# Queries and gates of a recurrence as seven half-size products, and state-space tiles activated as they are projected

## The chip, the cores and the metric

One NeuronCore of a Trainium2 chip runs the whole program. The metric is the device time of one execution in microseconds. Five engines work side by side: TensorE (PE, with its weight loads PEld), VectorE (DVE), ScalarE (ACT), GpSimd (POOL) and SyncE (SP), which here only issues transfers.

## The reference, cut to what matters

The program is three transformer-like blocks over 512 tokens of width 1024. The change lies in the third, all in fp32:

```
h = rmsnorm(x) * (1 + scale1) + shift1
z, xbc, dt, q, f_fwd, f_bwd, i, g = split(h @ w_in)
# state-space half
xbc = silu(conv5(xbc) + conv_b)                 # 1536 columns: 1024 x, 256 b, 256 c
y = x * d_skip + scan(x, b, c, dt) + reversed scan
y_ssd = rmsnorm(y * silu(z))
# gated linear recurrence half, for each direction d with f = f_fwd, f_bwd
log_f = logaddexp(log(lb), log1p(-lb) + log_sigmoid(f));  k = (1 - lb) * sigmoid(-f)
S_t = diag(f_t) S_{t-1} + k_t v_t^T;  o_t = S_t^T q_t           # v = i
y_hg = rmsnorm(o_fwd + o_bwd) * silu(g)
x = x + gate1 * (concat(y_ssd, y_hg) @ w_out)
```

`h @ w_in` for q and for g are two products of 1024 x 1024 by 1024 x 512 (features by tokens).

## The kernel before, in words

Activations lie in SBUF as tiles of 128 features by 512 tokens: `hT` is the normed input in eight such tiles, `xT` the residual stream. A `Stream` brings weights in pieces of 2 MB into two places; a piece is loaded into a place when the products that read the piece before it there are done (`products_to`). Each stage is a block: every engine has its own instruction list, the engines meet by semaphores, and a barrier stands at a block's end. Semaphores of closed blocks are cleared in bulk, with a barrier, when over 80 are used up (L126 to L136).

**State-space inputs** (`ssd_inputs`, L3196). TensorE makes twelve products (L3237) in eight PSUM banks; ScalarE copies each into a padded tile `raw` (L3252); VectorE does the convolution, one multiply and four multiply-adds a tile (L3269, L3272). When all twelve copies are issued, ScalarE applies Silu to the twelve tiles (L3257). Then a block of its own, `ssd_prepare` (L3287), turns the eight x tiles and two b tiles by transposes (L3308, L3311), makes the scores b'c (L3314), has ScalarE copy the twelve results out (L3321), and VectorE write `y = x * skip` (L3326). Two `ssd_direction` blocks follow.

**Inputs of the recurrence** (`hgrn_inputs`, L3517). TensorE makes five products of 8 banks each, in the order forget, back-forget, value, query, gate: a bank is 8 tiles of contraction (16 matmul records of 512 columns, L3578). ScalarE takes each bank to SBUF by `take` (L3587). Between the takes stand the steps of a chain that makes log f and k, first for one direction and then for the other: Abs, Exp, Ln, Abs, Exp, Exp of the kept part, Ln (L3594 to L3626), with VectorE's steps between (L3678 to L3703). The chain's scratch tiles `a` and `b` are the tiles of the gates and of the queries. So a query bank is taken only when VectorE has counted `done` for its tile (L3701), the last but one step of the second direction's chain, which goes tile by tile. The kept parts go to DRAM through a ring of two tiles by transfers that GpSimd issues (L3554); ScalarE waits for the ring.

**After it**: `hgrn_recurrence` (L3706), sixteen passes, during which SyncE loads a 256 KB row block `kept` for each pass two passes ahead; then `mixed_out` (L4006).

**`SevenProducts`** (L225) is used in `mixed_out` and elsewhere. A pair of output tiles (256 features by 512 tokens, contraction 1024) is split in halves each way and made by seven products of half size instead of eight: each is 4 tiles of contraction by 256 columns. Products 5, 6 and 7 need sums of weight quarters s1 to s4 (`weigh`, four VectorE operations of 128 x 512) and sums of input quarters t1 to t4 (`add_values`, one operation of 128 x 1024 each); product 4 needs t4, product 3 needs s4. ScalarE takes product 1 (`first_out`) and products 1+2 (`corner_out`); VectorE adds the rest (`join_first`, three operations, and `join_last`, two). Pairs listed in `whole` are made plainly; a pair in `eager` runs its products in the order 1, 2, 6, 7, 5, 4, 3, others 1, 6, 7, 5, 2, 4, 3. Pair n uses banks 4(n mod 2) to 4(n mod 2) + 3.

Of the kernel before, what the change touches and what calls it, by code (L numbers as in the profile page):

```python
# [22 lines left out]
P = 128  # L23
# [3172 lines left out]
def ssd_inputs(core, stream, hT, conv_w, conv_b, xbc, normed, steps, z_load):  # L3196
# [6 lines left out]
    PIECES = TILES // 4  # L3203
    with ExitStack() as ctx:
        (raw,) = bufs(nc, ctx, "si", raw=[P, XT, T + 2 * PAD])
        product = stream.product
        copied, padded, tap, convolved, activated = sems(
            nc, ctx, *(f"si_{s}" for s in ("copied", "padded", "tap", "convolved", "activated")))
# [15 lines left out]
        @block.tensor  # L3224
        def _(pe):
            for n in normed:
                n.sums(pe)
            steps.multiply(pe, hT, B[7], normed[-1])
            for n in range(TILES):
                if n % 4 == 0:  # L3230
                    w = stream.take(pe)
                if n == 7:
                    pe.wait_ge(steps.copied, 1)
                if n >= 8:
                    pe.wait_ge(copied, n - 7)
                for k in range(KT):
                    mm = nc.tensor.matmul(B[n % 8][:], w[:, k, (n % 4) * P:(n % 4 + 1) * P], hT[:, k, :],  # L3237
                                          start=(k == 0), stop=(k == KT - 1))
                mm.then_inc(product, 1)
                if n == 10:  # L3240
                    pe.wait_ge(copied, 10)
                    steps.turn(pe, B[0], B[1])

        @block.scalar
        def _(act):
            for n in normed:
                n.scalar(act)
            steps.take(act, B[7])
            steps.logs(act)
            for n in range(TILES):  # L3250
                act.wait_ge(product, n + 1)
                nc.scalar.copy(raw[:, n, PAD:PAD + T], B[n % 8][:]).then_inc(copied, 1)  # L3252
                if n == 3:
                    steps.decays(act)
            for n in range(XT):
                act.wait_ge(convolved, n + 1)
                nc.scalar.activation(xbc[:, n, :], xbc[:, n, :], ACT.Silu, bias=conv_b[:, n:n + 1]).then_inc(activated, 1)  # L3257

        @block.vector
        def _(dve):  # L3260
# [6 lines left out]
            for n in range(XT):  # L3267
                dve.wait_ge(copied, n + 1)
                nc.vector.tensor_scalar(xbc[:, n, :], raw[:, n, 0:T], conv_w[:, n, 0:1], None, ALU.mult).then_inc(tap, 1)  # L3269
                for j in range(1, SSD_CONV):  # L3270
                    dve.wait_ge(tap, (SSD_CONV - 1) * n + j)
                    nc.vector.scalar_tensor_tensor(  # L3272
                        out=xbc[:, n, :], in0=raw[:, n, j:j + T], scalar=conv_w[:, n, j:j + 1], in1=xbc[:, n, :],
                        op0=ALU.mult, op1=ALU.add).then_inc(convolved if j == SSD_CONV - 1 else tap, 1)
                if n == 3:
                    steps.weigh(dve)
            steps.place(dve, B[0], B[1])

# [6 lines left out]


def ssd_prepare(core, xbc, x_tm, b_tm, scores, y, skip, ident):  # L3287

    nc = core.nc
    B = core.bank  # L3290
    with ExitStack() as ctx:
        turned, copied, skipped = sems(nc, ctx, "sp_turned", "sp_copied", "sp_skipped")
        block = ctx.enter_context(nc.Block())

        outs = [(x_tm[:, n // 2, (n % 2) * 512:(n % 2 + 1) * 512]) for n in range(8)]
        outs += [b_tm[:, 2 * n:2 * n + 2, :].rearrange("p t c -> p (t c)") for n in range(2)]
        outs += [scores[:, g, :] for g in range(SSD_G)]

        @block.tensor
        def _(pe):  # L3300
            for n in range(12):
                if n >= 8:
                    pe.wait_ge(copied, n - 7)
                for j in range(4):
                    out = B[n % 8][:, j * P:(j + 1) * P]
                    if n < 8:
                        t, k = n // 2, 4 * (n % 2) + j
                        mm = nc.tensor.transpose(out, xbc[:, k, t * P:(t + 1) * P], ident[:])  # L3308
                    elif n < 10:
                        t, g = 2 * (n - 8) + j // 2, j % 2  # L3310
                        mm = nc.tensor.transpose(out, xbc[:, 8 + g, t * P:(t + 1) * P], ident[:])  # L3311
                    else:
                        g, cols = n - 10, slice(j * P, (j + 1) * P)
                        mm = nc.tensor.matmul(out, xbc[:, 8 + g, cols], xbc[:, 10 + g, cols], start=True, stop=True)  # L3314
                mm.then_inc(turned, 1)

        @block.scalar
        def _(act):
            for n in range(12):
                act.wait_ge(turned, n + 1)  # L3320
                nc.scalar.copy(outs[n], B[n % 8][:]).then_inc(copied, 1)  # L3321

        @block.vector
        def _(dve):
            for k in range(KT):
                nc.vector.tensor_scalar(y[:, k, :], xbc[:, k, :], skip[:, k:k + 1], None, ALU.mult).then_inc(skipped, 1)  # L3326
# [190 lines left out]
def hgrn_inputs(core, stream, hT, f, q, gate, v_tm, K, total, lower, y_ssd, zs, ssd_gain, ones, kept_dram):  # L3517
# [9 lines left out]
    with ExitStack() as ctx:  # L3527
# [6 lines left out]
         kept_log, apart, joined, logged, summed, totalled, shifted, done) = sems(  # L3534
# [3 lines left out]
                "shifted", "done")))  # L3538
        block = ctx.enter_context(nc.Block())
        base = stream.base()  # L3540
        FORGET, BACK, VALUE, QUERY, GATE = range(5)

        @block.sync
# [15 lines left out]
        def _(pe):  # L3559
            for i in range(5):  # L3560
                for s in range(2):
                    w = stream.take(pe)
                    for m in range(4):
# [15 lines left out]
                        mm.then_inc(stream.product, 1)  # L3579

        @block.scalar
        def _(act):
# [66 lines left out]
            for n in range(8):  # L3649
                act.wait_ge(done, n + 1)  # L3650
                take(QUERY, n, q[:, n, :], ACT.Identity)
            for n in range(8):
                act.wait_ge(joined, KT + n + 1)
                take(GATE, n, gate[:, n, :], ACT.Silu)

        @block.vector
        def _(dve):
# [14 lines left out]
            for d in range(2):  # L3672
# [12 lines left out]
                for k in range(KT):  # L3685
# [20 lines left out]
def hgrn_recurrence(core, q, sums, keys, totals, v_tm, y, ident, kept_dram, ahead):  # L3706
# [14 lines left out]
    with ExitStack() as ctx:  # L3721
# [5 lines left out]
         turned_copied, u_made, state, out_made, added, cleared, *kept_loaded) = sems(  # L3727
            nc, ctx, *(f"{name}_{s}" for s in (
                "loaded", "negated", "diffed", "q_exped", "k_exped", "scaled", "product", "picked", "zeroed", "started", "decayed", "end_diffed",
                "end_exped", "end_scaled", "turned", "turned_copied", "u_made", "state", "out_made", "added", "cleared",  # L3730
# [16 lines left out]
        def _(sp):  # L3747
            for d, levels in enumerate(("levels", "levels_back")):
                sp.dma_start(mask[:, d], core.const(levels)).then_inc(loaded, 16)
            for h in range(PASSES):  # L3750
                if h >= 2:
                    sp.wait_ge(product, NM * (h - 1))
                if h == HG_H + 2:
                    ahead(sp)
                sp.dma_start(kept[:, h % 2, :], kept_rows(kept_dram, h // HG_H, h % HG_H)).then_inc(kept_loaded[h % 2], 16)

# [438 lines left out]
def third_block(core, a, xT, hT, ident, ones, out):  # L4195
    nc = core.nc
    w_in = a["w_in_3"][0]
    with ExitStack() as ctx:
# [5 lines left out]
        hin = Stream(core, hin_ctx, "hin", 2, halves(w_in[:, 1024 + XBC + SSD_H:], (1, 2, 3, 0, 4)), first=zw[:])  # L4204
# [16 lines left out]
        with ExitStack() as s:  # L4221
            (ycat,) = bufs(nc, s, "b3", ycat=[P, 2 * KT, T])
            y_ssd, y_hg = ycat[:, 0:KT, :], ycat[:, KT:2 * KT, :]
            with ExitStack() as r:
                (zs,) = bufs(nc, r, "b3", zs=[P, KT, T])
                with ExitStack() as q:
                    xbc, *by_token = bufs(nc, q, "b3", xbc=[P, XT, T], dT=[P, TT, SSD_ROWS], shift=[P, TT, SSD_ROWS],
                                          WT=[P, TT, SSD_ROWS], CD=[P, TT, SSD_ROWS])
                    with ExitStack() as n:
# [5 lines left out]
                        ssd_inputs(core, si, hT, c["conv_w"], c["conv_b"], xbc, (n8, n9), steps, z_load)  # L4235
                    si_ctx.close()
                    b_tm, scores = bufs(nc, q, "b3", b_tm=[P, TT, SSD_G * P], scores=[P, SSD_G, T])
                    x_tm = y_hg.rearrange("p (t a) c -> p t (a c)", a=2)
                    ssd_prepare(core, xbc, x_tm, b_tm, scores, y_ssd, c["skip"], ident)
# [4 lines left out]
                with ExitStack() as q:  # L4244
                    ff, fb, kf = bufs(nc, q, "b3", ff=[P, KT, T], fb=[P, KT, T], kf=[P, KT, T])
                    v_tm = y_hg.rearrange("p (t a) c -> p t (a c)", a=2)
                    f, K, total = (ff, fb), (kf, zs), (c["total"], c["back_total"])
                    hgrn_inputs(core, hin, hT, f, hq, gs, v_tm, K, total, lower, y_ssd, zs, c["ssd_norm_w"], ones,
                                a["y_dram"])
# [7 lines left out]
                    hgrn_recurrence(core, hq, f, K, total, v_tm, hT, ident, a["y_dram"], first_out)  # L4257
# [34 lines left out]
def build(nc, a, out):  # L4292
    USED.clear()
    with ExitStack() as ctx:
# [13 lines left out]
        core.bias_stored, core.small_loaded, core.rest_loaded = (  # L4308
            ctx.enter_context(nc.semaphore(n)) for n in ("bias_stored", "small_loaded", "rest_loaded"))
# [35 lines left out]
```

## Time and profile before

| | us |
|---|---|
| median of 3 runs (lowest, highest) | 3619.79 (3616.84, 3621.1) |
| the profiled execution | 3621.61 |
| its span | 3619.4 |
| PE busy in the span | 3346.4 (92%) |
| DVE busy | 1600.5 (44%) |
| ACT busy | 765.7 (21%) |
| POOL busy | 266.4 (7%) |

The mean granted clock of TensorE was 0.95 of full speed. The span is the time from the first to the last instruction of the profiled execution; the rest lies around it. Times in the rows below count from the span's start.

### The profile page before, as it was taken

The page shows a single profiled execution, that of the slowest core. Times are in us where ns is not written, and L with a number is a line of the kernel's source. Part 1 is how long each engine was busy: PE and PEld are TensorE (multiplying, and loading weights), DVE is VectorE, ACT ScalarE, POOL GpSimd, SP SyncE. Part 2 cuts the span into 40 slices and gives each one's busy share as a digit, 9 for nine tenths or more (in the row PEclk, how much of TensorE's full clock was granted, in tenths as well). Part 3 has the DMA queues.
Part 4 walks back from the last instruction along what each step waited for, and adds up shares of the span by engine and source line. Part 5 has one row for each costly group of instructions (what it writes and reads, how often), then busy time and mean ns, then how long its engine had stood idle before and what let it go on. Part 6 is the DMA issues. An engine that isn't in the chain of part 4 may idle for free. (4 is left out here: it accounts for less than half of the span.)

```text
span 3619.4 us, 35011 instructions
## 1 busy us (share of the span) xinstructions
PE 3346.4 (92%) x12642; PEld 1891.8 (52%) x12642; DVE 1600.5 (44%) x2838; ACT 765.7 (21%) x1556; POOL 266.4 (7%) x372
## 2 busy tenths in 40 slices
PE   8995599999997899999999999698999998989998
PEld 3443247544474344444444444335544498868886
DVE  6882715893355111111111110556526288644553
ACT  1102312112113011010010010225544266120001
POOL 1000021000001000000000000100000187000000
PEclk9995699999998999999999999799999999999998
DMA  8860028212115999999999995413323101312220
GB/s 264 300 211 25 14 108 317 80 70 70 47 53 210 399 401 400 397 393 398 396 394 401 394 393 220 146 48 94 120 95 115 34 25 39 131 69 71 93 94 24
DMA packets 204253, 683.62 MB, mean 189 GB/s; under 512 B 15974, under 2 KB 27832, under 8 KB 171356
## 3 DMA queue, kind: packets, MB, share of 16 engines
q1 hardware_dynamic: 179340, 607.83, 44.7%
q0 software_dynamic: 14576, 48.71, 3.8%
q10 hardware_dynamic: 10208, 25.37, 1.9%
q8 instruction: 80, 1.31, 0.2%
q14 instruction: 49, 0.40, 0.0%
HBM read 628.63 MB, written 53.23 MB: 188 GB/s over the span
## 5 line engine op out<-in xcount | busy, mean ns | idle before, releaser
L2604 PE MATMUL bank<-moe_gu,all_hT 128*128 128x512 f32 x1024 | 445.2, 595 | 10.6 <-PEq L136 9.4
L2886 DVE TENSOR_SCALAR all_hT<-bank 128x512 f32<-128x512 f32 x48 | 33.2, 692 | 798.9 <-PE bank L2610 637.4
L2604 PEld LDWEIGHTS bank<-moe_gu,all_hT 128*128 128x128 f32 x1024 | 195.3, 191 | 256.2 <-issue 254.8
L2626 PE MATMUL bank<-moe_gu,all_hT 128*64 128x512 f32 x1024 | 222.6, 592 | 1.5 <-issue 1.5
L1922 PE MATMUL bank<-all_hT,early_w 128*128 128x512 f32 x512 | 220.2, 592 | 0.0
L2646 PE MATMUL bank<-moe_dn,moe_rows 128*128 128x512 f32 x480 | 210.0, 595 | 4.2 <-ACT moe_rows L2781 4.2
L1922 PEld LDWEIGHTS bank<-all_hT,early_w 128*128 128x128 f32 x512 | 97.3, 190 | 122.0 <-issue 122.0
L1984 DVE SCALAR_TENSOR_TENSOR b_conv<-conv_ya,all_table,b_conv 128x512 f32<-128x512 f32 x240 | 159.4, 748 | 0.0
L2626 PEld LDWEIGHTS bank<-moe_gu,all_hT 128*64 128x64 f32 x1024 | 76.4, 137 | 144.8 <-issue 144.8
L2646 PEld LDWEIGHTS bank<-moe_dn,moe_rows 128*128 128x128 f32 x480 | 90.0, 190 | 115.3 <-issue 107.6
L3956 PE MATMUL bank<-hg_qs,hg_ks 128*128 128x64 f32 x896 | 114.3, 279 | 19.7 <-ACT hg_ks L3845 13.8
L3956 PEld LDWEIGHTS bank<-hg_qs,hg_ks 128*128 128x128 f32 x896 | 110.9, 199 | 22.2 <-ACT hg_ks L3845 15.3
L3578 PE MATMUL bank<-all_hT,z_w 128*128 128x512 f32 x256 | 112.9, 602 | 4.8 <-PEq L3339 4.8
L397 PE MATMUL bank<-b_v,ff_S 128*128 128x256 f32 x496 | 117.2, 379 | 0.0
L3578 PE MATMUL bank<-all_hT,hin_w 128*128 128x512 f32 x256 | 110.5, 592 | 0.0
L2664 PE MATMUL bank<-moe_dn,all_hT 128*64 128x512 f32 x480 | 106.3, 595 | 0.8 <-ACT all_hT L2785 0.8
L1191 PE MATMUL bank<-all_hT,early_w 128*128 128x512 f32 x224 | 104.3, 624 | 0.8 <-DVE all_hT L800 0.8
L397 PEld LDWEIGHTS bank<-b_v,ff_S 128*128 128x128 f32 x496 | 94.2, 190 | 12.8
L2963 POOL DMA_INDIRECT combine_rows<-expert_rows,ex_row x16 | 17.6, 1102 | 1115.0 <-SPq L2948 1110.5
L2785 ACT COPY all_hT<-bank 128x512 f32<-128x512 f32 x16 | 9.4, 587 | 424.0 <-PE bank L2556 424.0
L3578 PEld LDWEIGHTS bank<-all_hT,z_w 128*128 128x128 f32 x256 | 49.5, 194 | 67.1 <-issue 67.1
L3237 PE MATMUL bank<-all_hT,si_w 128*128 128x512 f32 x192 | 82.9, 593 | 0.0
(837 smaller groups left out, 5389.2 us busy)
## 6 DMA issues: line engine op xcount, KB each, us to landing
moe_gu<-in_w_gu_dram SPq DMA_DIRECT2D x128, 2048.0 KB, 14.6
moe_dn<-in_w_dn_dram SPq DMA_DIRECT2D x62, 2048.0 KB, 14.2
early_w<-in_w_in_dram SPq DMA_DIRECT2D x13, 2048.0 KB, 9.0
expert_rows<-b_z POOLq DMA_DIRECT2D x49, 512.0 KB, 20.5
mods_w<-in_w_mod_dram SPq DMA_DIRECT2D x48, 512.0 KB, 5.3
mods_w<-in_ada_w_dram SPq DMA_DIRECT2D x48, 512.0 KB, 5.1
late_w<-in_w_up_dram SPq DMA_DIRECT2D x8, 2048.0 KB, 9.0
late_w<-in_w_down_dram SPq DMA_DIRECT2D x8, 2048.0 KB, 7.8
```

The lines of the kernel that those rows point to most:

```text
L397: mm = self.nc.tensor.matmul(self.bank(n, into), left[:, k, :], right[:, k, :], start=start and k == 0, stop=not start and k == 3, skip_gr ...
L1191: mm = nc.tensor.matmul(bank[:], w[:, k, at:at + P], hT[:, k, :], **flags)
L1922: mm = nc.tensor.matmul(bank(n)[:], w[:, k, (n % 4) * P:(n % 4 + 1) * P], hT[:, k, :], start=(k == 0), stop=(k == KT - 1))
L1984: nc.vector.scalar_tensor_tensor(out=conv[:, k, :], in0=ya[:, k, bass.ds(j, T)], scalar=conv_w[:, k, bass.ds(j, 1)], in1=conv[:, k, :], op ...
L2604: mm = nc.tensor.matmul(B[bank][:], xb2[:, k, :], gu[:, q, kk, col:col + HALF], start=(k == 0), stop=False)
L2626: mm = nc.tensor.matmul(B[bank][part, :], xb1[:, k % 4, k // 4, :], gu[:, 4 + q, kk, col + h * HALF:col + (h + 1) * HALF], start=(k == 0), ...
L2646: mm = nc.tensor.matmul(B[2 + n][:], left[:, k * P:(k + 1) * P], dn[:, c, j * D + n * HALF:j * D + (n + 1) * HALF], start=(k == 0), stop=( ...
L2664: mm = nc.tensor.matmul(B[4][part, :], hidT1[:, j, c, :], w[:, c, j * D + h * HALF:j * D + (h + 1) * HALF], start=(c == 0 and j == 0), sto ...
L2886: vec.tensor_scalar(g, gate[:], SWIGLU_LIMIT, None, ALU.min).then_inc(clipped, 1)
L3237: mm = nc.tensor.matmul(B[n % 8][:], w[:, k, (n % 4) * P:(n % 4 + 1) * P], hT[:, k, :], start=(k == 0), stop=(k == KT - 1))
L3578: mm = nc.tensor.matmul(B[n][:], left, right, start=(k == 0), stop=(k == KT - 1))
L3956: mm = nc.tensor.matmul(B[n % 4][:, c * w:(c + 1) * w], left[:, c * P:(c + 1) * P], right[:, c * w:(c + 1) * w], start=True, stop=True)
```

## The change

1. **Queries and gates.** In `hgrn_inputs` TensorE's plain loop stops after three products (forget, back-forget, value). Query and gate become eight pairs of a `SevenProducts`: pairs 0 and 1 (query tiles 0 to 3) plain, pairs 2 to 7 by seven products, pair 2 in the eager order. Pair 0 waits for 20 and pair 1 for all 24 of the banks taken before. The input sums are written over `y_ssd`'s first six tiles, the half sums over its last two, and the weight sums over `xT`. Both are stored to DRAM first: `xT` (2 MB) by SyncE at the block's start, ahead of the weight pieces; `y_ssd` (2 MB) by GpSimd when it is normed, ahead of the kept parts on GpSimd's queue. SyncE brings them back in the recurrence when its second and its third pass are done, each ahead of a `kept` row block. VectorE's sums stand in its list behind the whole chain of the second direction. The gate's Silu becomes an operation on the joined tile.
2. **State-space tiles.** Silu moves between the copies: tiles 0 to 3 after copy 4, tile n - 1 after copy n. `raw` has 8 tiles in place of 12. The block `ssd_prepare` is gone; its transposes, scores and copies run at the end of `ssd_inputs`, on six banks, one x tile after the other (the copy writes four pieces of 128 columns), and its `y = x * skip` behind VectorE's convolution. The last tile's Silu stands behind four of the copies.

```diff
 # ssd_inputs, TensorE, after the twelve products
+            for i in range(len(outs)):
+                if i < len(TURN_BANKS):
+                    pe.wait_ge(copied, max(n for n in range(TILES) if n % 8 == TURN_BANKS[i]) + 1)
+                else:
+                    pe.wait_ge(turned_copied, i - len(TURN_BANKS) + 1)
+                pe.wait_ge(activated, i + 1)
...
 # ssd_inputs, ScalarE
             for n in range(TILES):
                 act.wait_ge(product, n + 1)
-                nc.scalar.copy(raw[:, n, PAD:PAD + T], B[n % 8][:]).then_inc(copied, 1)
+                if n >= RAW:
+                    act.wait_ge(convolved, n - RAW + 1)
+                nc.scalar.copy(raw[:, n % RAW, PAD:PAD + T], B[n % 8][:]).then_inc(copied, 1)
                 if n == 3:
                     steps.decays(act)
-            for n in range(XT):
-                act.wait_ge(convolved, n + 1)
-                nc.scalar.activation(xbc[:, n, :], xbc[:, n, :], ACT.Silu, bias=conv_b[:, n:n + 1]).then_inc(activated, 1)
+                if n >= 4:
+                    for m in range(4) if n == 4 else [n - 1]:
+                        activate(m)
+            for i in range(len(outs)):
+                if i == LAST_AFTER:
+                    activate(TILES - 1)
+                act.wait_ge(turned, i + 1)
+                nc.scalar.copy(outs[i], turn_bank(i)[:].rearrange("p (t c) -> p t c", c=P)).then_inc(turned_copied, 1)
 # hgrn_inputs, SyncE and GpSimd
+            sp.dma_start(x_away, xT.rearrange("p k t -> p (k t)")).then_inc(x_stored, 16)
             stream.load(sp, 10)
+            pool.wait_ge(ssd_normed, KT)
+            pool.dma_start(y_away, y_ssd.rearrange("p k t -> p (k t)")).then_inc(core.y_ssd_stored, 16)
 # hgrn_inputs, TensorE
-            for i in range(5):
+            for i in range(3):
...
+            for n in range(own.count):
+                if n < 2:
+                    pe.wait_ge(copied, 2 * KT + 4 * (n + 1))
+                if n in own.whole:
+                    own.multiply_whole(pe, n)
+                else:
+                    own.multiply(pe, n, own.order(n))
 # hgrn_inputs, ScalarE, after the values
-            for n in range(8):
-                act.wait_ge(done, n + 1)
-                take(QUERY, n, q[:, n, :], ACT.Identity)
-            for n in range(8):
-                act.wait_ge(joined, KT + n + 1)
-                take(GATE, n, gate[:, n, :], ACT.Silu)
+            for n in own.whole:
+                act.wait_ge(done, 2 * n + 2)
+                own.whole_out(act, n)
+            for n in range(2, own.count):
+                own.first_out(act, n)
+                act.wait_ge(done, min(2 * n + 2, KT))
+                own.corner_out(act, n)
+                if n > 4:
+                    open_gate(n - 1)
+            open_gate(own.count - 1)
 # hgrn_inputs, VectorE, after the loop over both directions
+            dve.wait_ge(x_stored, 16)
+            dve.wait_ge(core.y_ssd_stored, 16)
+            for i in (0, 1, 3):
+                own.add_values(dve, 0, i)
+            own.weigh(dve, 2)
+            own.weigh(dve, 3)
+            dve.wait_ge(stream.product, own.base + 2)
+            own.add_values(dve, 0, 2)
+            for n in range(2, own.count):
+                own.join_first(dve, n)
+                own.join_last(dve, n)
+                if n + 2 < own.count:
+                    own.weigh(dve, n + 2)
 # hgrn_recurrence, SyncE, in the loop over passes
+                if h in (3, 4):
+                    to, away = back[h - 3]
+                    sp.dma_start(to.rearrange("p k t -> p (k t)"), away).then_inc(brought_back, 16)
```

`open_gate(n)` waits for the joined tiles of pair n and applies Silu to both.

## Rows read from the trace of the kernel before

**Rows 1.** windows: busy us of PE, PEld, DVE, ACT, POOL by stage, then clock
```profile
2452.10:2472.60 20.50, 8.86 (x57) 8.66 (x56) 7.81 (x17) 15.97 (x26) 0.00 (x0) 0.67 0.00 0
...
2590.50:2877.50 287.00, 284.07 (x656) 125.47 (x656) 101.08 (x157) 107.40 (x180) 8.79 (x17) 0.99 0.24 82
```

**Rows 2.** timeline, TensorE, inputs of the recurrence: start, duration, instruction, idle before
```profile
2593.11 30.00 PE L3578 MATMUL bank<-all_hT,z_w 128*128 128x512 f32 x64 [4.78 <-PEq L3339]
...
2739.68 27.63 PE L3578 MATMUL bank<-hin_w,all_hT 128*128 128x512 f32 x64
...
2767.15 27.63 PE L3578 MATMUL bank<-all_hT,z_w 128*128 128x512 f32 x64
...
2849.55 27.63 PE L3578 MATMUL bank<-all_hT,hin_w 128*128 128x512 f32 x64
```

**Rows 3.** timeline, VectorE, second direction's chain
```profile
2785.91 0.69 DVE L3688 SCALAR_TENSOR_TENSOR b_hq<-b_hq,b_gs 128x512 f32<-128x512 f32 x1 [26.35 <-ACT b_gs L3626]
...
2818.20 0.69 DVE L3703 TENSOR_TENSOR b_zs<-b_fb,b_zs 128x512 f32<-128x512 f32 x1
```

**Rows 4.** timeline, ScalarE, same stage: ring wait, last values, end
```profile
2775.05 0.63 ACT L3621 ACTIVATE hgate_kept<-b_zs 128x512 f32<-128x512 f32 x1 [7.24 <-DMA expert_rows<-hgate_kept]
...
2789.42 1.06 ACT L3587 ACTIVATE b_ycat<-bank 128x512 f32<-128x512 f32 x2
...
2877.28 0.60 ACT L3587 ACTIVATE b_gs<-bank 128x512 f32<-128x512 f32 x1 [6.27 <-PE bank L3578]
```

**Rows 5.** windows, TensorE after an idle stretch: busy us, granted clock, DMA
```profile
2593.00:2595.00 2.00, 1.89 (x3) 0.50 0.43 96
```

**Rows 6.** timeline, VectorE, sums of a seven-product stage after the recurrence
```profile
3072.60 0.69 DVE L431 TENSOR_TENSOR mx_S<-first_out_w 128x512 f32<-128x512 f32 x1 [1.54 <-PEq L136]
...
3074.53 0.69 DVE L436 TENSOR_TENSOR mx_S<-first_out_w,mx_S 128x512 f32<-128x512 f32 x1
...
3075.14 1.22 DVE L450 TENSOR_TENSOR b_zs<-b_ycat 128x1024 f32<-128x1024 f32 x1
...
3078.67 1.22 DVE L461 TENSOR_TENSOR b_zs<-b_ycat,b_zs 128x1024 f32<-128x1024 f32 x1
```

**Rows 7.** timeline, TensorE, first products of two consecutive pairs there
```profile
3143.66 1.89 PE L397 MATMUL bank<-b_ycat,late_w 128*128 128x256 f32 x8
...
3155.75 1.89 PE L397 MATMUL bank<-b_ycat,late_w 128*128 128x256 f32 x8
```

**Rows 8.** DMA issues of the page and of the inputs stage: KB each, us to landing
```profile
expert_rows<-b_z POOLq DMA_DIRECT2D x49, 512.0 KB, 20.5
...
expert_rows<-hgate_kept POOLq DMA_DIRECT2D x16, 256.0 KB, 2.3
```

**Rows 9.** timelines, VectorE and GpSimd: state-space result normed, first kept part stored
```profile
2635.47 5.39 DVE L3667 SCALAR_TENSOR_TENSOR b_ycat<-b_ycat,all_table,hgate_rstd 128x512 f32<-128x512 f32 x8
...
2697.28 1.15 POOL L3554 DMA_DIRECT2D expert_rows<-hgate_kept  x2 [104.11 <-ACT hgate_kept L3621]
```

**Rows 10.** timeline, all engines, end of the state-space inputs and the turning block
```profile
2452.18 0.59 ACT L3252 COPY si_raw<-bank 128x512 f32<-128x512 f32 x1 [8.24 <-PE bank L3237]
...
2453.32 3.11 DVE L3272 SCALAR_TENSOR_TENSOR b_xbc<-si_raw,all_table,b_xbc 128x512 f32<-128x512 f32 x4
...
2454.07 7.45 ACT L3257 ACTIVATE b_xbc<-b_xbc,all_table 128x512 f32<-128x512 f32 x12
...
2457.14 0.35 DVE L3193 COPY b_CD<-bank 128x192 f32<-128x192 f32 x1
...
2462.93 6.17 PE L3308 MATMUL bank<-all_ident,b_xbc 128*128 128x128 f32 x32 [10.80 <-PEq L136]
...
2462.94 3.26 DVE L3326 TENSOR_SCALAR b_ycat<-b_xbc,all_skip 128x512 f32<-128x512 f32 x8 [5.45 <-PEq L136]
...
2472.69 3.67 PE L3475 MATMUL bank<-all_hT,z_w 128*128 128x512 f32 x8 [0.93 <-PEq L3291]
```

**Rows 11.** timeline, SyncE's queue, same stage
```profile
2767.34 0.37 SPq L193 DMA_DIRECT2D hin_w<-in_w_in_dram  x1
```

More of the change, by code:

```diff
@@ L3242, in _ @@
                     steps.turn(pe, B[0], B[1])
+            for i in range(len(outs)):
[4 more added lines that the diff above has]
+                pe.wait_ge(activated, i + 1)
+                for t in range(TT):
+                    out, cols = turn_bank(i)[:, t * P:(t + 1) * P], slice(t * P, (t + 1) * P)
+                    if i < KT + SSD_G:
+                        mm = nc.tensor.transpose(out, xbc[:, i, cols], ident[:])
+                    else:
+                        mm = nc.tensor.matmul(out, xbc[:, i - SSD_G, cols], xbc[:, i, cols], start=True, stop=True)
+                mm.then_inc(turned, 1)
         @block.scalar
@@ L3277, in _ @@
             steps.place(dve, B[0], B[1])
+            for k in range(KT):
+                dve.wait_ge(activated, k + 1)
+                nc.vector.tensor_scalar(y[:, k, :], xbc[:, k, :], skip[:, k:k + 1], None, ALU.mult).then_inc(skipped, 1)
 def ssd_pieces(w_in):
@@ L3284, in ssd_pieces @@
     return [(v[:, :, col:col + HALF], 4) for col in cols]
[L3287 to L3326, printed above, removed]
 def ssd_direction(core, d, xbc, x_tm, b_tm, scores, columns, y, rows_dram, hT, zw, z_loaded, z_load, zs):
@@ L3537, in hgrn_inputs @@
                 "outer_term", "log_sig", "kept_log", "apart", "joined", "logged", "summed", "totalled",
-                "shifted", "done")))
-        block = ctx.enter_context(nc.Block())
+                "shifted", "done", "opened")))
+        (x_stored,) = sems(nc, ctx, "hgate_x_stored")
         base = stream.base()
         FORGET, BACK, VALUE, QUERY, GATE = range(5)
+        units = [dict(src=hT, into=lambda n: q[:, n % KT, :]), dict(src=hT, into=lambda n: gate[:, n % KT, :])]
+        own = SevenProducts(core, ctx, stream, "hgate", units, (SevenProducts.weights_within(xT),
+                                                                *SevenProducts.parts_within(y_ssd[:, 6:8, :])),
+                            (SevenProducts.values_within(y_ssd[:, 0:6, :]),), eager=[2], whole=[0, 1])
+        own.base, own.pieces = base + 3 * KT, stream.taken + 6
+        block = ctx.enter_context(nc.Block())
         @block.sync
@@ L3648, in _, with open_gate @@
                 take(VALUE, n, v_tm[:, n % 4, n // 4 * HALF:(n // 4 + 1) * HALF], ACT.Identity)
-            for n in range(8):
-                act.wait_ge(done, n + 1)
-                take(QUERY, n, q[:, n, :], ACT.Identity)
-            for n in range(8):
-                act.wait_ge(joined, KT + n + 1)
-                take(GATE, n, gate[:, n, :], ACT.Silu)
+            def open_gate(n):
+                own.joined(act, n)
+                for i in range(2):
+                    tile = own.units[n // 4]["into"](2 * n + i)
+                    func(tile, tile, ACT.Silu).then_inc(opened, 1)
+            for n in own.whole:
[8 more added lines that the diff above has]
+            open_gate(own.count - 1)
         @block.vector
```

57 lines of the change are left out of this document (37 added, 20 removed).

## The prediction

> **What bounds the kernel now.** I read the table of windows by stage first. TensorE sets the time almost everywhere, and the two stages that the change touches are opposites. In the turning block between the state-space inputs and the two directions TensorE is busy for 8.86 of 20.5 us; in the inputs of the recurrence it is busy for 284 of 287 us [rows 1]. So the first has time to give back by being laid beside other work, and the second by less TensorE work, as long as nothing else becomes late there.
>
> The engines' timelines of the second stage come next. TensorE runs its five products without a gap, four banks in 27.47 us (2767.15 - 2739.68), so a pair of banks takes 13.73 us; the last product starts its second half at 2849.55 and ends 27.47 us later, at 2877.02 [rows 2]. Beside it runs the chain for the forget gates, which is not bound by TensorE: VectorE starts its last part, eight tiles one after the other, at 2785.91 when ScalarE's last logarithm arrives, and ends at 2818.89 [rows 3]. The chain thus ends 58 us before TensorE does, and all of the query and gate work after 2767.15 is what hides it. ScalarE takes the queries as the chain frees their tiles, behind the last values at 2789.42 [rows 4]; that banks come round only every eighth product keeps this from TensorE.
>
> **Queries and gates, step by step**, in the clock of the trace before.
>
> - *Pair 0* runs plainly from 2767.15 to 2780.9.
> - *Pair 1* waits until all 24 banks are taken. The last two values are taken at 2789.42 to 2790.48, because the ring of kept parts and the last logarithms stand before them in ScalarE's list [rows 4]. TensorE idles 9.6 us, then works to 2804.2. After 4.78 us of idling its half clock (0.50) made four banks take 30.00 instead of 27.6 us [rows 2, 5]; with 2.4 us for that, pair 1 ends at 2806.6, and products 1 and 2 of pair 2, with ScalarE's copy between, at about 2810.5.
> - *Product 6 of pair 2* needs t2 and s2, which VectorE makes only behind the chain. It is busy to 2818.89. Three input sums, at the pace of the same sums in the later stage, take 3.53 us (3075.14 to 3078.67), to 2822.4; s1, s3 and s2 take 1.93 us (3072.60 to 3074.53), to 2824.3 [rows 3, 6]. So TensorE idles a second time, for 13.8 us. This wait swallows the one before pair 1 and its slow restart whole: neither is counted.
> - *Product 7* needs t3, which stands behind both sets of weight sums: 2 x 2.54 us from 2822.4, then 1.22, gives 2828.7 [rows 6]. Products 7, 5, 4 and 3 then take 4 x 1.73 us, since a pair's seven take 12.09 us (3155.75 - 3143.66) [rows 7]. That is 2835.7. The restart at half clock covers product 6, which has 4.4 us of room, and may reach into product 7: between 0 and 2.4 us by [rows 2, 5], of which I take 1.0, as much of it lies in the room. Pair 2 ends at 2836.7.
> - *Pairs 3 to 7*: 5 x 12.09 = 60.45 us, to 2897.1. VectorE needs about 5 us of each 12 for the joins (five additions of 0.4) and the next weight sums (2.54), and ScalarE under 3, so I add no wait; the weight pieces have some 24 us each.
> - *Tail*: before, one Silu of 0.60 us follows the last bank [rows 4]; now one VectorE addition (I take 0.4, half of the columns of a 0.69 operation [rows 6]) and two Silus follow: 1.0 us more.
>
> TensorE ends at 2897.1 instead of 2877.0, so the stage is longer by 20.1 + 1.0 = **21.1 us**. Seen as a balance: six pairs save 6 x (13.73 - 12.09) = 9.8 us of work; two idle stretches, the wait for t3 and restarts cost about 30.
>
> A rule of the Trainium skill speaks against the change here too: TensorE: Matmul & The Clock Gate, section HAM oscillation, says that idle gaps between bursts of matmuls put the engine back to half rate, so that a restart is paid after each. By it both gaps would cost a restart; the trace agrees for one gap (0.50 after 4.78 us). With the second restart at its full 2.4 us the sum would be 1.4 us higher, without any it would be 1.0 lower.
>
> *Transfers.* The store of `xT` stands ahead of the weight piece at 2593, which is not needed before TensorE has made four banks, 30 us later [rows 2]. The store of `y_ssd` stands on GpSimd's queue ahead of the kept parts. Its 2 MB bound from below by eight times the 256 KB that land in 2.3 us, 18 us, and from above by four times the 512 KB that took 20.5 us in the busiest stage, 82 us [rows 8]. The room is 56 us, from the last normed tile at 2635.47 + 5.39 = 2640.9 to the first kept part at 2697.3 [rows 9], so I take the near row, from this stage, and count nothing. The Trainium skill, DMA: Bandwidth & Descriptors, section on the anatomy of a DMA, gives a fit for GpSimd-issued copies, 2.0 us plus bytes over 436 000; that is an estimate of 6.8 us, and no delay either. In the recurrence the two loads of 2 MB precede row blocks that are needed a whole pass after the next; nothing counted, at most some us if they were late.
>
> **State-space tiles.** Before, the last Silu ends at 2454.07 + 7.45 = 2461.52, the barrier of the clearing costs 1.4 us, the turning block runs from 2462.93, and the first direction starts TensorE at 2472.69 [rows 10]. After, TensorE can turn tiles from 2452.2 on. ScalarE takes the last product to 2452.77, one Silu (0.62 at the row's pace) to 2453.4, four copies of 0.55 to 2455.6, waits for the last convolution, which ends at 2453.32 + 3.11 = 2456.43, makes its Silu to 2457.1 and eight copies of 0.55, to 2461.5 [rows 10]. VectorE places its four small copies (the last ends by 2457.5) and then needs 3.26 us for the skip, to 2460.8 [rows 10]. So the block ends when it ended before, and the turning block from 2462.93 to 2472.69 falls away: **-9.8 us**. The earlier Silus and their table load lie in ScalarE's idle time between the copies (8.24 us before the last [rows 10]). The barrier of the clearing moves on to the first direction; a second such barrier moves from the entry of `mixed_out` to that of the recurrence, for nothing. If the four-piece copies were slower, or TensorE restarted at half clock after its 3 us without work, up to 2.4 us of the gain are lost.
>
> **Sum.** 3621.6 + 21.1 - 9.8 = 3632.9 us against the profiled execution. The median of the runs is 1.8 us lower, so I forecast 3631 us, 11 us slower.
>
> **Rivals.**
>
> - *The sums come in time and TensorE stays the bound* (faster). Then the six pairs give back 9.8 us, the turning block 9.8, the tail costs 1.0: 3619.8 - 18.6 = 3601. It decides at about 2810: VectorE's sums would have to be made 14 us earlier. For it speaks that VectorE stands idle for 26.35 us before 2785.91; against it, that its list is in order and the sums stand behind the chain [rows 3]. Chance 0.09, with what I may have overlooked in that direction.
> - *The chain ends earlier.* ScalarE waits 7.24 us for the ring at 2775.05, because a weight piece was issued at 2767.34, just before the kept part [rows 4, 11]. With other transfers around it that wait may shrink, at most to nothing: the whole stage follows the chain now, so up to 7.2 us come off, 3624 to 3627, within 0.2% of before. The piece is still released by the end of the values, so little speaks for it. Chance 0.10.
> - *The store of `y_ssd` is late.* At 82 us it ends at about 2723, 26 us after the first kept part, which waits behind it, and the chain with it: 3657. Against it the row of this stage [rows 8]. Chance 0.03.
> - *The turning block's work does not fit* and its time is paid in the longer block: 3641. Chance 0.04.
>
> **How the numbers follow.** The forecast has 0.74, with a range of its own from 3627 to 3635: 1.0 less and 1.4 more for the restart, 2.4 for the turning block, about 2 for the runs' own spread. A measurement of this kernel can tell about 0.2%, 7.2 us, from no change. Faster: 0.09. Same: the shorter chain, 0.10, and the forecast's low edge, 0.05. Slower: the rest, 0.76. The range goes from 3622, through the shorter chain, to 3638, through half of the turning block's rival.
>
> **What would show it.** Right: in TensorE's timeline two gaps in the query stage, the longer one ended by VectorE's weight sums; the chain's last operation as late after the stage's start as before (226 us); six pairs of 12.1 us; the stage some 21 us longer; the first direction 9.8 us earlier after the last state-space product. Wrong: no second gap, or the sums ahead of the chain's end; a transfer as the releaser of a kept part beyond 7 us; the recurrence longer by more than 2 us; or copies of the turned tiles well over 0.6 us.

## The result, and the profile after

The changed kernel's median is 3627.9 us (14 runs, 3619.2 to 3631.8) against 3616.8 us of the kernel before on the same chip (14 runs): a ratio of 1.0027, 95% interval 1.0020 to 1.0035. That is 11.1 us slower, where 3631 us and 11.3 us slower had been forecast. Of the 3.1 us between 3631 and 3627.9, 3.0 come from the base: the kernel before has a median of 3616.8 us here and had 3619.8 in the three runs from which the forecast went out. The profiled execution took 3628.9 us, with a span of 3627.1.

First the windows of the two stages that the change touches, as in [rows 1], and TensorE's window behind the second gap, to set beside [rows 5] (stretch, its length, busy us of PE, PEld, DVE, ACT and POOL with their counts, granted clock, DMA share, GB/s).

```profile
2449.40:2459.90 10.50, 6.53 (x57) 6.11 (x56) 7.72 (x17) 7.75 (x15) 0.00 (x0) 1.00 0.00 0
...
2579.60:2885.60 306.00, 280.05 (x800) 154.72 (x800) 131.27 (x212) 109.51 (x188) 9.32 (x18) 0.96 0.26 90
...
2810.50:2812.50 2.00, 1.96 (x5) 1.60 (x6) 1.98 (x4) 0.00 (x0) 0.00 (x0) 0.50 0.00 0
```

The state-space stage's end has shrunk from 20.5 to 10.5 us. The inputs of the recurrence have grown from 287 to 306 us although TensorE is busy for 4 us less in them: what the longer stage holds is idle time.

TensorE's timeline of the query and gate products shows it (start, duration, instruction, and in brackets the idle time before and what ended it). [Rows 2] had no idle time here.

```profile
2753.99 13.90 PE L352 MATMUL bank<-all_hT,z_w 128*128 128x512 f32 x32
2776.69 17.05 PE L352 MATMUL bank<-all_hT,z_w 128*128 128x512 f32 x32 [8.80 <-ACT b_ycat L3597]
2793.57 1.89 PE L397 MATMUL bank<-all_hT,hin_w 128*128 128x256 f32 x8
2795.93 1.99 PE L397 MATMUL bank<-all_hT,hin_w 128*128 128x256 f32 x8 [0.46 <-ACT b_ycat L405]
2810.54 3.47 PE L397 MATMUL bank<-b_ycat,all_xT 128*128 128x256 f32 x8 [12.62 <-DVE all_xT L434]
2815.03 1.97 PE L397 MATMUL bank<-all_hT,all_xT 128*128 128x256 f32 x8 [1.01 <-DVE all_hT L458]
...
2822.01 1.89 PE L397 MATMUL bank<-all_hT,hin_w 128*128 128x256 f32 x8
...
2880.71 1.89 PE L397 MATMUL bank<-all_hT,all_xT 128*128 128x256 f32 x8
```

The values end at 2753.99, pair 0 runs, and TensorE waits 8.80 us for ScalarE's last value copy. It then does pair 1 and two products of pair 2, and waits 12.62 us for the weight sum s2 on VectorE and 1.01 us more for t3. From 2822.01 on there is no idle time: the five pairs 3 to 7 take 60.4 us, to 2882.44. Read as a balance, the eight pairs took 109.9 us before (2877.02 - 2767.15) and take 128.45 now. Six pairs save 9.8; the four idle stretches add 22.9; half clock after them adds 3.15 to pair 1 and 1.6 to product 6; 0.8 is left for modelled ends and slightly longer first products.

VectorE's timeline names the cause of the long gap; compare [rows 3, 6].

```profile
2772.07 0.69 DVE L3708 SCALAR_TENSOR_TENSOR b_hq<-b_hq,b_gs 128x512 f32<-128x512 f32 x1 [25.98 <-ACT b_gs L3636]
...
2804.34 0.69 DVE L3723 TENSOR_TENSOR b_zs<-b_fb,b_zs 128x512 f32<-128x512 f32 x1
2804.95 1.22 DVE L450 TENSOR_TENSOR b_ycat<-all_hT 128x1024 f32<-128x1024 f32 x1
...
2807.46 1.22 DVE L461 TENSOR_TENSOR b_ycat<-all_hT,b_ycat 128x1024 f32<-128x1024 f32 x1
2808.60 0.68 DVE L431 TENSOR_TENSOR all_xT<-hin_w 128x512 f32<-128x512 f32 x1
...
2809.81 0.68 DVE L434 TENSOR_TENSOR all_xT<-all_xT,hin_w 128x512 f32<-128x512 f32 x1
...
2813.66 1.22 DVE L458 TENSOR_TENSOR all_hT<-all_hT 128x1024 f32<-128x1024 f32 x1
...
2882.64 0.42 DVE L485 TENSOR_TENSOR b_gs<-b_ycat,bank 128x256 f32<-128x256 f32 x1 [1.30 <-PE bank L397]
```

VectorE idles 25.98 us before the chain's last part, makes the chain without a break to 2805.03, and only then the input sums (L450 to L461) and the weight sums (L431 to L436). TensorE's product 6 starts 0.05 us after the sum of L434 is made. The chain ends 225.4 us after the stage's first product, where it ended 225.8 after it before.

ScalarE in the same stage, beside [rows 4]: the wait for the ring of kept parts, the last two values, and the end.

```profile
2759.36 0.63 ACT L3631 ACTIVATE hgate_kept<-b_zs 128x512 f32<-128x512 f32 x1 [5.02 <-DMA expert_rows<-hgate_kept]
...
2775.58 1.05 ACT L3597 ACTIVATE b_ycat<-bank 128x512 f32<-128x512 f32 x2
...
2883.18 1.15 ACT L3663 ACTIVATE b_gs<-b_gs 128x512 f32<-128x512 f32 x2 [2.52 <-DVE b_gs L485]
2885.63 1.28 ACT L3832 ACT_TABLE_LOAD   x1 [1.31 <-PEq L136]
```

The ring's wait is 5.02 us instead of 7.24. At the end two Silus follow the last join, and then 1.31 us of the semaphore-clearing barrier; the recurrence's first instruction comes 3.2 us behind TensorE's end, where it came 1.1 us behind it.

The moved transfers, from the DMA issues of the stretch from 2570 to 3080 (KB each, us to landing).

```profile
expert_rows<-all_xT SPq DMA_DIRECT2D x1, 2048.0 KB, 8.8
h_rows<-b_ycat POOLq DMA_DIRECT2D x1, 2048.0 KB, 6.6
all_xT<-expert_rows SPq DMA_DIRECT2D x1, 2048.0 KB, 8.0
b_ycat<-h_rows SPq DMA_DIRECT2D x1, 2048.0 KB, 7.6
```

All four land in under 9 us; none of them ends a wait in the timelines above.

The turning block, all engines, beside [rows 10].

```profile
2449.35 4.53 PE L3259 MATMUL bank<-all_ident,b_xbc 128*128 128x128 f32 x40
2449.55 0.59 ACT L3280 COPY si_raw<-bank 128x512 f32<-128x512 f32 x1 [7.63 <-PE bank L3244]
...
2450.66 2.04 ACT L3290 COPY b_ycat<-bank 128x512 f32<-128x512 f32 x4
...
2453.84 0.72 ACT L3272 ACTIVATE b_xbc<-b_xbc,all_table 128x512 f32<-128x512 f32 x1 [1.15 <-DVE b_xbc L3305]
...
2457.32 1.12 ACT L3290 COPY b_scores<-bank 128x512 f32<-128x512 f32 x2
...
2459.93 3.67 PE L3469 MATMUL bank<-all_hT,z_w 128*128 128x512 f32 x8 [2.79 <-PEq L136]
```

TensorE turns tiles directly behind the last product, ScalarE's copies of the turned tiles take 0.51 us each (2.04 / 4), and the first direction starts 10.38 us after the start of the last product's copy (2459.93 - 2449.55), where it was 20.51 (2472.69 - 2452.18).

Put together, stage by stage, from the two profiled executions:

| stretch | before | after | difference | forecast |
|---|---|---|---|---|
| up to the first state-space product (not touched) | 2367.5 | 2364.9 | -2.6 | 0 |
| from there to the last state-space copy | 84.7 | 84.7 | 0.0 | 0 |
| last state-space copy to first direction | 20.51 | 10.38 | -10.1 | -9.8 |
| the two directions | 120.4 | 119.7 | -0.7 | 0 |
| inputs of the recurrence, TensorE's start to end | 283.9 | 302.8 | +18.9 | +20.1 |
| from there to the recurrence's first instruction | 1.1 | 3.2 | +2.1 | +1.0 |
| rest of the span | 741.3 | 741.5 | +0.2 | 0 |

Without the first line, which lies ahead of the change and is between 2359 and 2368 us in all the profiled executions of this study, the sum is +10.4 us; the medians differ by 11.1, the forecast was +11.3.

### The profile page after: what moved, and what is told of

The parts are those of the page before. It is cut to its first block and busy times, and to the rows that moved or that the text cites. A ratio compares the mean times of both kernels' runs of the same rounds, so it can differ in the third digit from the quotient of the medians.

```text
span 3627.1 us, 35437 instructions
## 1 busy us (share of the span) xinstructions
PE 3338.8 (92%) x12786; PEld 1918.2 (53%) x12786; DVE 1631.7 (45%) x2896; ACT 766.8 (21%) x1564; POOL 266.6 (7%) x373
## 5 line engine op out<-in xcount | busy, mean ns | idle before, releaser
L2604 PE MATMUL bank<-moe_gu,all_hT 128*128 128x512 f32 x1024 | 445.2, 595 | 10.4 <-PEq L136 9.3
L2604 PEld LDWEIGHTS bank<-moe_gu,all_hT 128*128 128x128 f32 x1024 | 195.4, 191 | 256.1 <-issue 254.7
L3993 PE MATMUL bank<-hg_qs,hg_ks 128*128 128x64 f32 x896 | 114.4, 279 | 21.6 <-ACT hg_ks L3882 13.7
L2891 DVE TENSOR_TENSOR all_hT<-all_hT,moe_hid 128x512 f32<-128x512 f32 x32 | 22.2, 693 | 136.8 <-ACT moe_hid L2776 136.8
L397 PE MATMUL bank<-b_z 128*128 128x256 f32 x312 | 70.7, 379 | 0.6 <-DVE b_z L458 0.6
## 6 DMA issues: line engine op xcount, KB each, us to landing
expert_rows<-b_z POOLq DMA_DIRECT2D x49, 512.0 KB, 20.5
```

Source lines behind the costliest of these rows:

```text
L397: mm = self.nc.tensor.matmul(self.bank(n, into), left[:, k, :], right[:, k, :], start=start and k == 0, stop=not start and k == 3, skip_gr ...
L2604: mm = nc.tensor.matmul(B[bank][:], xb2[:, k, :], gu[:, q, kk, col:col + HALF], start=(k == 0), stop=False)
L2891: after(vec.tensor_tensor(g, g, hid, ALU.mult), 2)
L3993: mm = nc.tensor.matmul(B[n % 4][:, c * w:(c + 1) * w], left[:, c * P:(c + 1) * P], right[:, c * w:(c + 1) * w], start=True, stop=True)
```

## Experiments

Each was timed against the kernel before on the same chip; e1 to e4 ran together on one chip, e5 and e6 on a second, e7 on a third. The code shown is cut from the difference to the changed kernel. "Stage" is the time from the first product of the recurrence's inputs to the recurrence's first decay activation; it is 286.3 us before and 307.3 after.

**e1: the state-space part alone.** The inputs of the recurrence are those of before.

```diff
-            for i in range(3):
+            for i in range(5):
...
+            for n in range(8):
+                act.wait_ge(done, n + 1)
+                take(QUERY, n, q[:, n, :], ACT.Identity)
```

> The state-space part of the change alone; queries, gates and the recurrence as before. If the turning block's work fits into the end of the inputs' block, the first direction starts 10 us earlier after the last state-space copy (20.5 us before, 10.4 in the changed kernel's trace) and the time is 9.8 to 10.1 us below before, ratio 0.9972 to 0.9973. If the trace's difference was an accident of that execution or is given back in the two directions, ratio 0.999 to 1.001.

Measured: 3605.2 us against 3618.2, ratio 0.9962 (0.9949 to 0.9975). The expected ratio lies in the interval, near its slow end. In the trace it is 10.37 us from the last state-space copy to the first direction, as in the changed kernel, and the stage takes 286.4 us, as before. So the part is worth 10 us where it stands; the other 3 of the 13 us by the medians belong to no stage that the edit touches, and lie within the interval.

```profile
2445.98 0.59 ACT L3280 COPY si_raw<-bank 128x512 f32<-128x512 f32 x1 [7.63 <-PE bank L3244]
...
2456.35 3.67 PE L3469 MATMUL bank<-all_hT,z_w 128*128 128x512 f32 x8 [2.79 <-PEq L136]
```

**e2: the queries and gates alone.** The state-space part is that of before.

```diff
-                if n >= RAW:
-                    act.wait_ge(convolved, n - RAW + 1)
...
+            for n in range(XT):
+                act.wait_ge(convolved, n + 1)
```

> The query and gate part alone, with the turning block as before. If the two parts add up: 19 to 21 us above before, ratio 1.0053 to 1.0058. If the gates' part is cheap and the changed kernel lost its time elsewhere (transfers of the two moved tiles in the recurrence, the moved clearing), ratio under 1.003.

Measured: 3636.5 us, ratio 1.0057 (1.0045 to 1.0069), as expected, with gaps of 8.57 and 12.69 us in the trace. The stage takes 306.75 us. The two parts add up: by their places in the traces, -10.1 (e1) and +20.4 (306.75 - 286.3) make +10.3 us; by the ratios, -13.7 and +20.6 make +6.9, with some 6 us of uncertainty, beside +9.8 for both together by the ratio of 1.0027.

**e3: the sums ahead of the chain's last part.** The input sums t1, t2 and t4 and the weight sums of pairs 2 and 3 are made in VectorE's idle time; only t3 stays behind the chain. `weigh` drops a wait for these two pairs (not shown), as the plain pairs ahead of them use no weight sums.

```diff
+                if d:
+                    dve.wait_ge(x_stored, 16)
+                    dve.wait_ge(core.y_ssd_stored, 16)
+                    for i in (0, 1, 3):
+                        own.add_values(dve, 0, i)
+                    own.weigh(dve, 2)
+                    own.weigh(dve, 3)
...
-            own.weigh(dve, 2)
-            own.weigh(dve, 3)
```

> The changed kernel with three input sums and the weight sums of pairs 2 and 3 made ahead of the last part of the second direction's chain, in the 26 us in which VectorE waits there; only t3 stays behind the chain, since it overwrites input that the plain pairs read. If the sums' place behind the chain is what TensorE waits for: product 6 of pair 2 follows product 2 at once, product 7 starts 1.3 us after the chain's end instead of 10.0, and the time is 7 to 9 us below the changed kernel, ratio to before 1.000 to 1.001. If the sums push the chain back instead (the weights of pairs 2 and 3 land some 10 us before its last part starts, five operations must fit), the chain ends later by what does not fit and less is won. If the restarts at half clock and the wait before pair 1 are what costs, nothing changes: 1.0027.

Measured: 3621.1 us, ratio 1.0011 (1.0002 to 1.0020), 0.0001 above the expected range of 1.000 to 1.001, most of which lies in the interval. The stage takes 300.0 us: 7.3 of the 21.0 us have come back. First VectorE's timeline, then TensorE's.

```profile
2743.28 1.23 DVE L462 TENSOR_TENSOR b_ycat<-all_hT,b_ycat 128x1024 f32<-128x1024 f32 x1
2758.82 0.69 DVE L432 TENSOR_TENSOR all_xT<-hin_w 128x512 f32<-128x512 f32 x1 [14.32 <-DMA hin_w<-in_w_in_dram]
...
2763.28 0.69 DVE L437 TENSOR_TENSOR all_xT<-hin_w,all_xT 128x512 f32<-128x512 f32 x1
2766.83 0.69 DVE L3716 SCALAR_TENSOR_TENSOR b_hq<-b_hq,b_gs 128x512 f32<-128x512 f32 x1 [2.85 <-ACT b_gs L3637]
```

```profile
2771.45 16.83 PE L353 MATMUL bank<-all_hT,z_w 128*128 128x512 f32 x32 [8.91 <-ACT b_ycat L3598]
...
2792.30 1.89 PE L398 MATMUL bank<-b_ycat,all_xT 128*128 128x256 f32 x8
2801.07 3.65 PE L398 MATMUL bank<-all_hT,all_xT 128*128 128x256 f32 x8 [6.88 <-DVE all_hT L459]
2804.56 1.89 PE L398 MATMUL bank<-b_ycat,all_xT 128*128 128x256 f32 x8
```

The sums fit into the idle time: even after a wait of 14.32 us for the weight piece, 2.85 us were left before the chain's last part, which still waits for ScalarE. Product 6 now runs at once, at 2792.30, and product 7 waits 6.88 us for t3, made behind the chain. It is the place of the sums in VectorE's list that made the second gap, not VectorE's amount of work.

**e4: the first gap alone.** Pair 1 waits only for the two value tiles whose banks it takes over.

```diff
-                if n < 2:
-                    pe.wait_ge(copied, 2 * KT + 4 * (n + 1))
+                if n < 3:
+                    pe.wait_ge(copied, 2 * KT + (4, 6, 8)[n])
```

> The changed kernel with pair 1 waiting for six of the value banks, those up to the two it writes, instead of all eight; the wait for all eight moves to pair 2. If the second wait swallows the first: the first gap shrinks from 8.8 to 2 to 3 us, product 6 of pair 2 starts as late as before, and the time is that of the changed kernel within 1 us (ratio to before 1.0027). If every gap costs by itself, 6 us less: 1.0010.

Measured: 3628.8 us, ratio 1.0036 (1.0023 to 1.0049). TensorE's timeline:

```profile
2767.21 14.00 PE L352 MATMUL bank<-all_hT,z_w 128*128 128x512 f32 x32 [2.33 <-ACT b_ycat L3597]
...
2786.37 3.59 PE L397 MATMUL bank<-all_hT,hin_w 128*128 128x256 f32 x8 [3.43 <-ACT b_ycat L405]
2807.60 3.78 PE L397 MATMUL bank<-b_ycat,all_xT 128*128 128x256 f32 x8 [17.65 <-DVE all_xT L434]
2812.08 3.75 PE L397 MATMUL bank<-all_hT,all_xT 128*128 128x256 f32 x8 [0.70 <-DVE all_hT L458]
2815.63 2.54 PE L397 MATMUL bank<-b_ycat,all_xT 128*128 128x256 f32 x8
```

The first gap falls from 8.80 to 2.33 us, and the time moves into the waits behind it, 3.43 and 17.65: nothing is won, as forecast where the first gap was called swallowed. The stage is 2.0 us longer than in the changed kernel (309.3), which the expectation did not have: product 7 (3.75 us, granted clock 0.50) and part of the product after it run at half clock too.

**e5: four pairs plain.** Pairs 0 to 3, all of the queries, run plainly; the sums for the gates are made behind the chain, but beside two plain pairs.

```diff
-                                                                eager=[2], whole=[0, 1])
+                                                                eager=[4], whole=[0, 1, 2, 3])
```

> The changed kernel with four pairs plain instead of two: all queries plainly by pairs, the gates by seven products, weight sums for pairs 4 and 5. If TensorE's wait for the sums is the loss: it makes pairs 2 and 3 plainly in the time in which it idled, reaches the gates at about 27.5 us after the end of pair 1, finds the sums nearly ready, and ends the stage some 13 us earlier than the changed kernel although it does 3.3 us more work: ratio to before 0.999. If seven products save as such, two pairs fewer of them cost 3.3 us: 1.0036.

Measured: 3616.8 us, ratio 0.9994 (0.9984 to 1.0004); stage 294.25. TensorE's timeline:

```profile
2460.44 5.18 PE L3469 MATMUL bank<-all_hT,z_w 128*128 128x512 f32 x8 [2.79 <-PEq L136]
...
2778.45 16.91 PE L352 MATMUL bank<-all_hT,z_w 128*128 128x512 f32 x32 [8.66 <-ACT b_ycat L3597]
2795.19 27.63 PE L352 MATMUL bank<-all_hT,hin_w 128*128 128x512 f32 x64
...
2826.84 1.89 PE L397 MATMUL bank<-b_ycat,all_xT 128*128 128x256 f32 x8
```

The second gap is gone, although now only four pairs, not six, save TensorE work: the plain pairs cover the chain's end and the sums. What is left over the stage of before, 7.9 us, is the first gap (8.66), its slow restart (16.91 - 13.90 = 3.0), the 0.46 and the tail (2.1), less the 6.56 us that four pairs save: 7.7.

**e6: queries as before, on eight banks in turn, gates by seven products**, with the state-space part. Neither gap has a cause here: the query products lie between the values and the gates, and the sums are made beside them.

```diff
-        units = [dict(src=hT, into=lambda n: q[:, n % KT, :]), dict(src=hT, into=lambda n: gate[:, n % KT, :])]
+        units = [dict(src=hT, into=lambda n: gate[:, n, :])]
...
-            for i in range(3):
+            for i in range(4):
...
+            for n in range(8):
+                act.wait_ge(done, n + 1)
+                take(QUERY, n, q[:, n, :], ACT.Identity)
```

> All queries plainly on eight banks in turn, as before, and only the gates by seven products; the state-space part as in the change. If both gaps were from the pairs' waits: TensorE runs without a gap to the end of the queries, 55 us after the values, the chain and the first sums end at the same time within 2 us, and four pairs of 12.1 us follow: 6.2 us less than before in TensorE's end, 1.0 back in the tail, 9.8 to 10.1 from the state-space part: 15 us below before, ratio 0.9958. If moving two tiles out and back or the restarts cost what is not seen in the stage, ratio 0.998 or more.

Measured: 3604.5 us against 3618.2, ratio 0.9957 (0.9941 to 0.9972): it beats the kernel before, and by its ratio the changed one. TensorE idles for no longer than 0.46 us between the first product of the stage and the last. Its timeline of the gates:

```profile
2809.19 1.89 PE L397 MATMUL bank<-all_hT,z_w 128*128 128x256 f32 x8
2811.55 1.99 PE L397 MATMUL bank<-all_hT,z_w 128*128 128x256 f32 x8 [0.46 <-ACT b_ycat L405]
...
2856.54 1.89 PE L397 MATMUL bank<-all_hT,all_xT 128*128 128x256 f32 x8
```

Four pairs take 49.1 us (2809.19 to 2856.54 + 1.73) instead of 54.9; the tail takes 2.1 back, and the stage is 282.7 us, 3.6 less than before.

**e7: the same without the state-space part**, to see what seven products are worth where they stand free.

```diff
-                if n >= RAW:
-                    act.wait_ge(convolved, n - RAW + 1)
...
+            for n in range(XT):
+                act.wait_ge(convolved, n + 1)
...
-        units = [dict(src=hT, into=lambda n: q[:, n % KT, :]), dict(src=hT, into=lambda n: gate[:, n % KT, :])]
+        units = [dict(src=hT, into=lambda n: gate[:, n, :])]
```

> State-space part as before; queries plainly on eight banks in turn, as before, and only the gates as seven half-size products. My theory: the seven products themselves pay and the loss lay in the two gaps alone. Then there is no gap beyond 0.5 us here, the four pairs take 49 instead of 55 us on TensorE (2809.19 to 2858.27 in the run with both parts), the tail with its moved barrier gives back about 2, and the stage is 3.7 us shorter than before: ratio about 0.999 (0.9985 to 0.9995). Rival: the moved stores, loads and joins cost as much elsewhere as the products save (the recurrence longer by 2 us or more), and all of the gain of that other run is the state-space part's: ratio 1.000 or above.

Measured: 3615.2 us against 3618.6, ratio 0.9992 (0.9983 to 1.0001). By the time alone the rival's 1.000 is not excluded. The places in the traces speak against it. The stage is 282.1 us, 4.2 less than before; 0.4 of that is a shorter restart at its start (29.58 us for the first four banks instead of 30.00). The recurrence behind it, from its first decay activation to the first weight sum of the output stage, takes 192.1 us (193.2 before, 193.5 after; between 191.9 and 195.4 in e1 to e6). One execution proves little at this spread, but the seven with the moved tiles have a mean of 193.2 us, and the two without them (193.2 before, 194.6 in e1) one of 193.9: no price of 2 us shows. In TensorE's timeline

```profile
2817.41 1.89 PE L397 MATMUL bank<-all_hT,z_w 128*128 128x256 f32 x8
2819.76 1.99 PE L397 MATMUL bank<-all_hT,z_w 128*128 128x256 f32 x8 [0.46 <-ACT b_ycat L405]
...
2864.75 1.89 PE L397 MATMUL bank<-all_hT,all_xT 128*128 128x256 f32 x8
```

the four pairs take 49.1 us again. e1's 0.9962 times 0.9992 is 0.9954, beside e6's 0.9957. Whether e6 is faster than e1 their intervals don't tell; that it is by 3.7 us rests on the stage.

## Why the prediction was right

Times are from the end of the values (2767.15 before, 2753.99 after), which is where the forecast's working began.

| step | forecast | measured |
|---|---|---|
| pair 1 starts | 23.3 | 22.7 |
| pair 1 ends | 39.5 | 39.6 |
| chain ends | 51.7 | 51.0 |
| product 6 starts | 57.2 | 56.55 |
| product 7 starts | 61.6 | 61.0 |
| pair 2 ends | 69.6 | 68.0 |
| pair 7 ends | 130.0 | 128.45 |

The stage came out 21.0 us longer, where 21.1 was forecast. The mechanism was right; that the sum is so close is luck, since two errors cancel: TensorE's end came 1.2 us earlier than forecast (18.9 us instead of 20.1), and the tail cost 1.1 us more (2.1 instead of 1.0). In the working itself, 2835.7 for the end of pair 2's products adds up to 2835.6.

- *Two gaps, the second ended by the weight sums, and the first swallowed by it*: shown, by the timeline and by e4, where taking 6.5 us off the first gap shortened nothing.
- *The chain as late as before*: shown. It ends 225.4 us after the stage's first product instead of 225.8, and 0.7 us earlier than forecast after the end of the values. Of the 0.7 us, 0.3 are TensorE's: its restart at the stage's start took 30.30 us for four banks instead of 30.00, so the values end later. The ring's first wait shrank from 7.24 to 5.02 us, but those that follow grew from 4.5 us in all to 6.5, so that the ring costs 11.5 us of waiting instead of 11.8. A weight piece still goes out 0.2 us after the end of the values. The rival of the shorter chain thus came to about 0.3 of its at most 7.2 us.
- *Restart at half clock*: mis-sized twice. Pair 1's restart cost 3.15 us instead of 2.4, and counted for nothing, as it lies before the second gap. The 1.0 us that I let the second restart reach into product 7 did not occur: at a granted clock of 0.50 in its first 2 us product 6 took 3.47 us and still ended 1.01 us before product 7 could start, and product 7 ran in 1.97. That 1.0 us stood on no row: of the 4.4 us of room, product 6 left 2.7 (4.4 - 1.73), more than the 2.4 of a whole restart. It was no empty fear either, as in e4 product 7 was caught (3.75 us). The granted clock is 0.50 right behind the gaps of 8.80, 12.62, 6.88 (e3) and 17.65 us (e4), and 1.00 behind the one of 2.33 us in e4. The Trainium skill, TensorE: Matmul & The Clock Gate, section HAM oscillation, has the engine back at half rate after idle gaps; the trace agrees for the first four. Whether the time counts depends on what waits next: in the changed kernel it did not.
- *Six pairs at 12.09 us*: five pairs took 60.43 us where 60.45 was forecast, and VectorE's joins and ScalarE's copies made no wait.
- *Tail*: forecast 1.0, measured 2.1. The join and the second Silu cost the 1.0. The other 1.04 is the barrier of the semaphore clearing, which I had moved "for nothing": it stands bare at the recurrence's entry (1.31 us of idle, where ScalarE idled for 0.27 us before). The idle time before the output stage's first weight sum fell from 1.54 to 0.32 us in exchange, but the recurrence as a whole is not shorter (193.2 and 193.5 us), so that gain could not be told from its spread.
- *Transfers*: nothing, as taken. The store of `y_ssd` was bounded by 18 and 82 us from [rows 8]; it landed in 6.6 us, below both: here neither eight rows of 256 KB nor four of 512 KB gave the price of one of 2 MB. The fit in the Trainium skill, DMA: Bandwidth & Descriptors, section on the anatomy of a DMA, gave an estimate of 6.8 us, and the trace agrees. The rival of the late store had no ground at all.
- *State-space tiles*: -10.1 against -9.8. The copies took 0.51 instead of 0.55 us. TensorE's first eight products of the first direction took 3.67 us after 2.79 us of idling, no longer than before [rows 10], so the restart that I had kept in the range did not occur; in one of the other executions, e5's, it did (5.18).
- *Sums in time*, the faster rival: it had 3601 us with its condition met. The condition can't be met by the sums' place alone, since t3 and the first gap remain (e3). Where both causes are gone part of that gain is there: e6 reached 3604.5, with four pairs by seven products, whose share (3.7 us) rests on the stage in the traces.

## What to carry to other kernels

Work that is cut from the bounding engine can be what hides another engine's chain: before cutting it, read when that chain ends and what the new work needs from it. An operand made by an in-order engine is as late as everything before it in that engine's list; place it in the idle stretch ahead of the chain (e3: 7.3 us off the stage), or give the cheaper form only to the products whose operands are ready (e5, e6). Where a change has two independent parts, time each alone: here one was worth -0.4% and the other cost +0.6%.

## What was not expected of the hardware

- One store of 2 MB issued by GpSimd landed in 6.6 us, though the 512 KB stores of a stretch with a DMA share of 1.00 (523 to 613 us in the kernel before) took 20.5 and those of 256 KB beside it 2.5: neither the small nor the contended transfers of this case gave the price of the large one.
- After the 17.65 us gap of e4 half clock lasted through two products and part of a third (3.78, 3.75 and 2.54 us instead of 1.89; granted clock 0.50, 0.50 and 0.73), though a wait of 0.70 us lay between; after 12.62 us in the changed kernel and 6.88 in e3 only one product was slow (3.47 and 3.65). Before its long gap e4's TensorE had also run one product at half clock (3.59 us, after 3.43 us of idling). What decides between the two was not tried.
